# One transfer per expert instead of two, and one wait before its issue

## What is computed

```python
aff = sigmoid(xt @ router)                 # xt (320, 1024), router (1024, 32)
eidx = top 2 experts inside the best group # then gate = normalised weights, (320, 32)
hg = silu(xt @ w_gate[e]) * (xt @ w_up[e]) # w_gate, w_up (1024, 256) for each of 32 experts
hg = hg * gate[:, e]
out = out + hg @ w_down[e]                 # w_down (256, 1024)
```

## Time and profile before

| | us |
|---|---|
| time, median of 3 executions | 1628.29 (1626.69 to 1629.29) |
| time of the profiled execution | 1637.19 |
| its span, first to last instruction | 1635.4 |
| mean granted clock of TensorE, share of full speed | 0.800 |
| PE busy | 1252.9 (77%) |
| DVE, ACT, POOL busy | 452.3, 194.8, 162.8 |
| moved by DMA | 309.57 MB, of it 201.3 MB of experts |

### The profile page before, as it was taken

The page is one execution under the profiler, slowest core; times in us unless marked ns, Lnnn a source line. Parts: engine busy times, 40 slices in busy tenths (PEclk is TensorE's granted clock), DMA queues, the critical chain, the costliest instruction groups (busy, mean ns, idle before and its releaser), DMA issues. The chain is left out here.

```text
span 1635.4 us, 14202 instructions
## 1 busy us (share of the span) xinstructions
PE 1252.9 (77%) x4976; PEld 693.7 (42%) x4976; DVE 452.3 (28%) x1090; ACT 194.8 (12%) x423; POOL 162.8 (10%) x205
## 2 busy tenths in 40 slices
PE   7999766689979937888874189779989559887860
PEld 5777555566643333333331045545564243232320
DVE  0067554433441052111111512221110431111115
ACT  0111112100020011110100113221110111101100
POOL 0000024311000021101010100000000111011101
PEclk9999857655569956998997589596668759999995
DMA  5234420004232333999995500504414418999952
GB/s 221 103 134 170 178 90 1 26 27 143 89 118 79 152 135 112 423 423 422 416 420 205 210 24 1 156 19 116 133 41 180 180 46 365 421 424 421 416 226 103
DMA packets 52971, 309.57 MB, mean 189 GB/s; under 512 B 12722, under 2 KB 17714, under 8 KB 30898
## 3 DMA queue, kind: packets, MB, share of 16 engines
q1 hardware_dynamic: 41490, 290.44, 44.7%
q0 software_dynamic: 9216, 10.51, 1.9%
q10 hardware_dynamic: 2208, 7.87, 1.4%
HBM read 300.61 MB, written 31.23 MB: 203 GB/s over the span
## 5 line engine op out<-in xcount | busy, mean ns | idle before, releaser
L1033 PE MATMUL ps<-ring,xsT 128*64 128x512 f32 x1024 | 250.6, 646 | 64.5 <-DMA ring<-in_experts 62.9
L285 PE MATMUL ps<-XT,ring 128*128 128x320 f32 x640 | 175.5, 438 | 11.2 <-DMA ring<-in_w_in 11.2
L1033 PEld LDWEIGHTS ps<-ring,xsT 128*64 128x64 f32 x1024 | 87.3, 149 | 226.0 <-issue 223.6
L285 PEld LDWEIGHTS ps<-XT,ring 128*128 128x128 f32 x640 | 123.2, 193 | 63.0 <-issue 13.4
L1058 PE MATMUL ps<-ring,hT 128*64 128x512 f32 x512 | 116.9, 598 | 16.5 <-DVE hT L1268 16.5
L1266 DVE TENSOR_TENSOR hid<-sg,ps 128x256 f32<-128x256 f32 x32 | 13.5, 421 | 303.9 <-ACT sg L1088 303.9
L805 PE MATMUL ps<-ring,zT 128*128 128x512 f32 (+1 forms) x192 | 87.8, 605 | 0.0
L885 PE MATMUL ps<-C,X 128*128 128x128 f32 (+1 forms) x72 | 15.1, 391 | 93.3 <-POOL X L854 93.3
L1130 POOL DMA_INDIRECT y_dram<-ys,index x32 | 32.2, 1005 | 427.4 <-DVE ys L1274 427.4
L1058 PEld LDWEIGHTS ps<-ring,hT 128*64 128x64 f32 x512 | 33.9, 136 | 79.0 <-issue 54.9
L854 POOL TENSOR_TENSOR X<-X,lnp 128x1024 f32<-128x1024 f32 (+1 forms) x12 | 28.0, 2336 | 364.3 <-DVE X L847 364.3
(11 more groups left out here) (276 smaller groups left out, 1560.3 us busy)
## 6 DMA issues: line engine op xcount, KB each, us to landing
ring<-in_experts SPq DMA_DIRECT2D x64, 2048.0 KB, 19.8
ring<-in_experts SPq DMA_DIRECT2D x64, 1024.0 KB, 21.3
ring<-in_w_in SPq DMA_DIRECT2D x10, 2048.0 KB, 7.8
ring<-in_latent SPq DMA_DIRECT2D x48, 256.0 KB, 2.8
ring<-in_w_out SPq DMA_DIRECT2D x4, 2048.0 KB, 12.6
ring<-in_state SPq DMA_DIRECT2D x4, 1024.0 KB, 6.9
out_ssds<-ring SPq DMA_DIRECT2D x4, 1024.0 KB, 4.3
lnp<-in_ln SPq DMA_DIRECT2D x4, 1024.0 KB, 5.6
```

The costliest lines, as they stand in the source:

```text
L285: mm = pe.matmul(ps[:, q, 0:TOK], ring[:, u, k * 512 + q * P:k * 512 + (q + 1) * P], XT[:, k, :], start=(k == 0), stop=(k == KD - 1))
L1033: mm = pe.matmul(ps[e * SLOTS:(e + 1) * SLOTS, GU[p], :].rearrange("p (g f) -> p g f", g=2), xsT[:, p, k, e * SLOTS:(e + 1) * SLOTS], w[:, ...
```

## The change

The two helpers go. `first_expert` now issues one transfer of a whole slot, 24 KB per partition, with one semaphore per slot. The loop of SP issues both experts of a pair once `down` of pair `j - 2` is done, and no longer waits for `gate_up`. `gate_up(j)` waits for the whole experts; `down(j)` waits for no weights any more. The number of bytes is the same.

```diff
-        expert_in = [sems(f"expert_in{layer}_", 8) for layer in range(2)]
+        expert_in = [sems(f"expert_in{layer}_", 4) for layer in range(2)]
...
-        def load_gate_up(sp, layer, i):
-
-            sp.dma_start(ring[:, i % 4, 0:2 * KD * FF],
-                         a["experts"][layer * EXPERTS + i][:, 0:2 * KD * FF]).then_inc(expert_in[layer][i % 4], 16)
-
-        def load_down(sp, layer, i):
-
-            sp.dma_start(ring[:, i % 4, 2 * KD * FF:WEXP],
-                         a["experts"][layer * EXPERTS + i][:, 2 * KD * FF:WEXP]).then_inc(expert_in[layer][4 + i % 4], 16)
-
         def first_expert(sp, layer, i):
 
-            load_gate_up(sp, layer, i)
-            load_down(sp, layer, i)
+            sp.dma_start(ring[:, i % 4, :], a["experts"][layer * EXPERTS + i]).then_inc(expert_in[layer][i % 4], 16)
...
-                gu_in, d_in = expert_in[layer][:4], expert_in[layer][4:]
+                weights_in = expert_in[layer]
...
                         for j in range(2, PAIRS):
-                            sp.wait_ge(gu_done, j - 1)
-                            load_gate_up(sp, layer, 2 * j)
-                            load_gate_up(sp, layer, 2 * j + 1)
                             sp.wait_ge(d_done, j - 1)
-                            load_down(sp, layer, 2 * j)
-                            load_down(sp, layer, 2 * j + 1)
+                            first_expert(sp, layer, 2 * j)
+                            first_expert(sp, layer, 2 * j + 1)
...
-                            pe.wait_ge(gu_in[2 * p + e], 16 * (j // 2) + 16)
+                            pe.wait_ge(weights_in[2 * p + e], 16 * (j // 2) + 16)
...
                         pe.wait_ge(ht_copied, j + 1)
-                        for e in range(2):
-                            pe.wait_ge(d_in[2 * p + e], 16 * (j // 2) + 16)
...
-                        for done in in_window + gu_in + d_in:
+                        for done in in_window + weights_in:
                             pool.sem_clear(done)
```

## The result

The changed kernel takes 1675.6 us (median; 1666.33 to 1679.76), the kernel before 1628.8 us in the same comparison: a ratio of 1.028, 95% interval 1.0235 to 1.0325, so +46.8 us. The profiled execution of the changed kernel took 1679.8 us with a span of 1677.9, 42.5 us more than the span of the earlier trace rows. I forecast +34.8 us and 1663 us; the direction held, the size was a quarter short, and the median lies 0.6 us above the top of my range. Lines of the changed kernel have other numbers: its gate/up matmuls are L1019 (before: L1033), its down matmuls L1042, and SP's loads stand at L203. The counts behind an x are records of the trace. A float32 matmul stands as two records, so the 32 of gate/up in a pair are 16 matmuls and the 16 of down are 8; the description of the kernel before counts records there.

The account below looks back on a forecast made before the run. The weight stream was taken as the bound in the MoE. Terms 5.5 + 4.9 + 6.5 + 0.7 - 0.2 = +17.4 us per layer, +34.8 for two, gave 1663 us against the median of 1628.3; 8-in-10 range 1647 to 1675.

Parts of the forecast that it names:

- (a): Start of each MoE: pair 2's first load goes out after down of pair 0, not its gate/up; +5.5 us per layer.
- (b): End of each MoE: gate/up of pair 15 begins only after the last down weights land; +4.9 us per layer.
- (c): Pairs 2 to 13: loads issued after down leave holes in the stream when PE is slow; +6.5 us per layer.
- second rival: MoE pairs: PE starts slow in every pair, the shallow queue costing +14 us per layer; 1681 us, 10%.
- (d): Last pair: its gate/up may start slow after a longer stop; +0.7 us per layer, between 0 and 2.9.
- (e): SP, PE and POOL: fewer issues, waits and semaphore clears, gathers staying hidden; -0.2 us per layer.
- (f): Expert loads: 24 KB rows instead of 16 and 8 KB could move faster; taken as 0.
- first rival: MoE pairs: the shallow queue costs nothing, +20.6 us in all; 1649 us, 25%.

Follow-up runs that it names:

- head_late: Kernel before, only pair 2's gate/up loads wait for down of pair 0 instead of its gate/up: 1646.2 us, ratio 1.0118.
- wait_all: Kernel before with its early issue, but gate/up also waits for its pair's down weights: 1642.2 us, ratio 1.0108.
- after_warm2: Changed kernel plus 3 constant matmuls (6 before pair 2) between down and the next weight wait: 1663.5 us, ratio 1.0196.
- after_plus: Changed kernel with 4 added matmuls (3.6 us) ahead of each down, except pair 0: 1702.6 us, ratio 1.0442.
- late_two: Changed kernel's issue order and waits, but each expert as two transfers with two semaphores: 1679.2 us, ratio 1.030.
- late_split: Kernel before, all loads of a pair issued after down of pair j - 2, two transfers per expert, gate/up waiting for gate/up alone: 1643.8 us, ratio 1.0081.
- the quiet ones: Changed kernel and kernel before, each without gathers of pairs 2 to 15 and with all scatters after the last pair: medians 1691.3 and 1636.3 us.
- after_quiet: Changed kernel without gathers of pairs 2 to 15, all scatters after the last down (results wrong): 1691.3 us.
- after_warm: Changed kernel plus 6 constant matmuls (14 before pair 2) between down and the next weight wait: 1713.8 us.

## Why the prediction was right or wrong, point by point

**(a) Later start of the stream: right.** +5.5 forecast, +5.4 and +5.2 measured alone (`head_late`). In the changed kernel pair 2's first issue is at 646.07, with down of pair 0, and PE stood 6.14 us before gate/up of pair 2.

**(b) Wait for the down weights: right.** +4.9 forecast, +4.2 and +4.8 measured alone (`wait_all`). In layer 0 of the changed kernel the last load lands at 865.7 + 19.9 = 885.6 and gate/up of pair 15 starts at 885.92.

**(c) The shallow queue: right in mechanism, short in size.** +6.5 per layer forecast. What is left of the stretches after (a) and (b) is 22.6 - 5.4 - 4.2 = 13.0 and 21.4 - 5.2 - 4.8 = 11.4 us. What was off in both layers is PE's part c, the time from gate/up of a pair to the issue of the pair after next. I read seven slow groups of twelve in the kernel before (the timeline has six), spread slow starts over half the pairs with c around 14.3, and let them cost about 1.1 us each. In the changed kernel they stand in every even pair and in no odd one, and c is larger: 14.4 to 15.5 us in layer 0 (pair 2: 680.1 - 664.58 = 15.5; mean of pairs 2 to 12: 14.8), 15.2 on average in layer 1. Long stop, slow start, late issue, empty queue and long stop again follow each other through the even pairs, so the slow starts sit just where the loop has no reserve. The Trainium skill (TensorE: Matmul & The Clock Gate, HAM oscillation) tells of one part of this cycle, a wait for data and then a slow start, in every tile, and it was the mechanism of my second rival; it came true for one pair in two.

The time in an empty queue was as forecast in layer 1 (18.6 us on average over pairs 4 to 14, against 18.7) and half a microsecond longer in layer 0 (19.2, from 18.6 to 19.8). The loop is 14.8 + 19.2 + 0.3 = 34.3 us in layer 0 and 15.2 + 18.6 + 0.3 = 34.1 in layer 1, which is what two pairs take. Above the 32.2 us of an unbroken stream that is 2.1 and 1.9 us for each of six loops, +12.8 and +11.2 us, 12.0 on average. Of the 6.3 us beyond my figure in layer 0, about half is the higher c and half the queue time; the 4.7 us in layer 1 are all c. `after_warm2` and `after_plus` show that c works through this loop, in both directions, and that part of any change in c comes back as time in the queue or as clock; `late_two` against `late_split` shows that the loop binds only with (b) in place.

**(d) The last pair: wrong, small.** Pair 15 is odd, comes after a stop of 0.41 us and runs at full clock: 0 instead of +0.7. In `wait_all`, after a stop of 2.69 us, it did start slow.

**(e) Fewer instructions: right.** From the last scatter to SP's first issue after it:

```profile
900.04 0.97 POOL L1114 DMA_INDIRECT y_dram<-ys,index  x1 [11.93 <-DVE ys L1258]
...
904.52 0.33 SPq L1296 DMA_DIRECT2D ring<-in_w_dqkv  x1
```

4.48 us against 5.07, so -0.6 instead of -0.2 for four clears fewer, within its bound. This is no chance of one execution: the same distance is 5.07 or 5.08 us in all eight traces with 24 clears (the quiet ones aside) and 4.48 or 4.49 us in all four with 20, about 0.15 us for a clear. PE waited for a gather only before the first pair of each layer, 4.3 and 4.2 us, as before. The prediction has each gather asked for more than 20 us ahead; for pairs 3 and 4 it was 16.4 us, still longer than the 15.1 us in which the slowest landed.

**(f) Larger transfers: right, to about 0.2 us a pair.** An expert alone landed in 10.1 us, as in the earlier trace rows, and `late_two` has the same times with smaller parts. Where a pair was issued well ahead it came in 15.85 us instead of 16.05, and without the indirect DMAs in 14.60 (`after_quiet`) instead of 14.76. Transfer form and order of issue both differ there, so the 1% is not shown to be the form's. The fit of 2.0 us plus bytes that the prediction quotes is one that the Trainium skill (DMA: Bandwidth & Descriptors, Anatomy of one DMA) gives for DMAs that GpSimd issues; these loads come from SP, and the 4 us a pair worked out from it do not show in `late_two`.

In sum, with (c) from the loop, 5.3 + 4.5 + 12.0 - 0.6 = 21.2 us a layer, 42.4 in all, where the spans differ by 42.5; the forecast had 17.4 a layer. The first rival (the shallow queue costs nothing) fell. The range was too narrow on top because its forecast took (c) between 3 and 10 us, on slow starts scattered over the pairs. The 12 us that came are near the 14 of my second rival, in which all pairs start slow, since half of them, all in the same loop, are enough.

## What to carry to other kernels

When one buffer's release starts the next load, write the loop down: work on the buffer, issue to landing in an empty queue, restart. The double buffer here was free of holes only while this was shorter than two loads in a full queue, with some lead to spare: in `after_warm2` pairs issued 4.2 us or more before the queue ran dry landed within half a microsecond of the full queue's beat, those with about 3 us up to 2.1 us behind it. Merging the transfers was harmless in itself here; what cost time is that the merged one must wait for its last reader and makes its first reader wait for its last byte, and the two together cost about twice the sum of each alone (44.0 against 21.2 us). And look at who sits in the tight loop: a slow start of TensorE that was free under a full queue cost time once the issue of the next load hung on it.

## What the runs showed of the hardware

A float32 matmul of 128x128 by 512 columns stands as two records and takes 0.89 us at full clock (`after_warm`); the 64-wide ones of gate/up take 0.44 each (32 records, so 16 matmuls, in 7.09 us). The small indirect DMAs cost the weight stream 1.3 us per 0.33 MB (16.05 us a pair against 14.76). A pair of experts issued about 3 us before the one ahead of it had landed arrived 15.9 to 18.2 us after it, where the full queue has 16.05. And each semaphore that GpSimd clears at the end of an MoE cost about 0.15 us (5.07 against 4.48 us for four).
